# Joined: gate-row weights stacked as halves, a new order of the beginning, and turned weights evicted ahead of exponentials in the attention stage, with one weight split moved inside

## The reference, cut to what matters

```python
proj = x @ w_in                       # 1024 tokens, 1024 -> 5640 columns
(r_q, r_k, r_v, r_z, s_u, s_z, m_x, m_v, m_o, m_z, m_i, m_f, a_q, a_z) = split(proj)
...
y = gelu(y); s5o = y * sigmoid(y @ w_glu) * silu(s_z)          # S5 group, end of it
...
ig = m_i + ml_b_ig                                             # 4 gate rows
lf = log_sigmoid(m_f + ml_b_fg)                                # 4 gate rows
...
mk, mv = split(mem @ xa_w_kv)                                  # 256 memory tokens
s = einsum('blhd,bmhd->bhlm', a_q, mk) * XA_DH ** -0.5
xa = einsum('bhlm,bmhd->blhd', softmax(s), mv)                 # 4 heads
```

## Time and profile before

| | us |
|---|---|
| median of 3 runs | 1795.42 (1793.71 to 1797.22) |
| the profiled execution | 1792.38 |
| its span, first to last instruction | 1790.5 |
| PE busy | 1743.9 (97%) |
| DVE, ACT, POOL busy | 1026.6, 590.1, 545.0 |

### The profile page before, as it was taken

How to read it: one execution, slowest core, us unless ns; L and a number is a source line. 1 busy time by engine, 2 the same in 40 slices (tenths; PEclk the granted TensorE clock), 3 DMA queues, 4 the chain that set the end, 5 groups by cost and what they waited for, 6 DMA issues and landing times.

```text
span 1790.5 us, 22903 instructions
## 1 busy us (share of the span) xinstructions
PE 1743.9 (97%) x8880; PEld 1447.8 (81%) x8880; DVE 1026.6 (57%) x2018; ACT 590.1 (33%) x825; POOL 545.0 (30%) x354
## 2 busy tenths in 40 slices
PE   6999998999999999999999999989999999999998
PEld 6778886888787888888888788878887878888886
DVE  7899625562374378339747886243623925872524
ACT  5333343451124213432144332445211251143320
POOL 2553304022121413245455442130221131223451
PEclk9999999999999999999999999999999999999999
DMA  7334354042023206674433433640410322167451
GB/s 281 133 116 132 116 204 165 36 126 87 25 71 135 101 25 216 209 277 169 140 130 123 130 114 98 231 157 36 130 48 26 106 105 95 50 224 281 177 174 58
DMA packets 98707, 235.23 MB, mean 131 GB/s; under 512 B 10912, under 2 KB 41968, under 8 KB 97064
## 3 DMA queue, kind: packets, MB, share of 16 engines
q1 hardware_dynamic: 72744, 183.20, 30.2%
q10 hardware_dynamic: 25776, 50.34, 7.7%
q0 software_dynamic: 80, 0.23, 0.0%
HBM read 170.55 MB, written 58.98 MB: 128 GB/s over the span
## 4 chain that ended last, share of the span: by engine, by line
PE 81%; DVE 7%; DMA 4%; ACT 3%; POOL 2%; issue 1%; SPq 0%; ACTq 0%; DVEq 0%
PE gp L628 20%; PE gp L630 19%; PE gp L629 19%; PE mm L628 3%; PE mm L629 3%; PE mm L630 3%; POOL wlo L1144 2%; DMA wraw<-in_w 2%; PE mm L856 1%; PE mm L834 1%; PE mm L783 1%; DMA yraw<-yt 1%; PE mm L784 1%; PE mm L785 1%; PE mm L996 1%
## 5 line engine op out<-in xcount | busy, mean ns | idle before, releaser
L1144 POOL TENSOR_TENSOR wlo<-wraw,whi 128x256 fp32r<-128x256 f32 (+1 forms) x282 | 450.8, 1624 | 1037.6 <-ACT whi L1221 1037.4
L628 PE MATMUL gp<-xh,whi 128*128 128x512 f32 x768 | 320.3, 417 | 2.0 <-ACT xh L1288 1.1
L630 PE MATMUL gp<-xh,wlo 128*128 128x512 f32 x768 | 301.8, 393 | 0.0
L629 PE MATMUL gp<-xl,whi 128*128 128x512 f32 x768 | 300.7, 392 | 0.0
L628 PE MATMUL gp<-whi,xh 128*128 128x512 f32 x640 | 269.0, 420 | 0.0
L1221 ACT ACTIVATE whi<-wraw 128x1024 fp32r<-128x1024 f32 x164 | 168.2, 1054 | 294.4 <-DMA wraw<-in_w 132.2
L630 PE MATMUL gp<-whi,xl 128*128 128x512 f32 x640 | 250.5, 391 | 0.0
L629 PE MATMUL gp<-wlo,xh 128*128 128x512 f32 x640 | 250.0, 391 | 0.0
L630 PEld LDWEIGHTS gp<-xh,wlo 128*128 128x128 f32 x768 | 144.8, 189 | 32.1
L628 PEld LDWEIGHTS gp<-xh,whi 128*128 128x128 f32 x768 | 145.4, 189 | 31.1 <-issue 4.4
L629 PEld LDWEIGHTS gp<-xl,whi 128*128 128x128 f32 x768 | 145.7, 190 | 25.8
(11 more groups left out here) (333 smaller groups left out, 2942.0 us busy)
## 6 DMA issues: line engine op xcount, KB each, us to landing
wraw<-in_w SPq DMA_DIRECT2D x164, 512.0 KB, 4.1
spill<-gate ACTq DMA_DIRECT2D x32, 512.0 KB, 2.9
yraw<-yt SPq DMA_DIRECT2D x32, 512.0 KB, 5.5
xs<-xr SPq DMA_DIRECT2D x16, 512.0 KB, 5.4
xraw<-in_xT SPq DMA_DIRECT2D x4, 1024.0 KB, 17.9
ud<-gate ACTq DMA_DIRECT2D x8, 512.0 KB, 2.6
uu<-ud SPq DMA_DIRECT2D x64, 64.0 KB, 2.5
p_tab<-kd SPq DMA_DIRECT2D x64, 64.0 KB
```

The source lines that it names most:

```text
L628: nc.tensor.matmul(out, ah, bh, start=start, stop=False)
L629: nc.tensor.matmul(out, ah, bl, start=False, stop=False)
L630: return nc.tensor.matmul(out, al, bh, start=False, stop=stop)
L1144: last = nc.gpsimd.tensor_tensor(wlo[slot(u)][:, w0 + c:w0 + c + n], raw_view(l, u, i)[:, c:c + n], whi[slot(u)][:, w0 + c:w0 + c + n].bit ...
```

## The change

Four things.

1. **Gate rows.** `wif` is now held as one weight `wifs`: in each group of 128 columns, the high part stands in columns 0 to 63 and the low part in 64 to 127. Two matmuls (with the high and the low part of x) take the place of three, and leave the low weight's products in rows 64 to 67 and 96 to 99 of the result. ACT copies those rows out (`rowl`), and DVE adds them, two operations put between its third and fourth rotary operation. The order on ACT is rowb, a wait for the attention's last store (`xo_out`), the low rows of it, rowi, its low rows, and a wait for DVE's first addition, then abs, exp, ln.
2. **Attention.** In a hook that has both, ACT evicts turned weights ahead of exponentials. Of the split of U_QK + 1 the first half now stands in the U_GL + 1 part and the second at hook 7 of U_QK. ACT's first two stores of the S5 output stand after the evictions of U_GL + 1, and the second two at the hook of the first values. DVE's last product of the S5 gate stands behind the first maximum. U_QK leaves `SMALL_STEPS`.
3. **The beginning.** ACT issues the two loads of the memory; SP issues the S5 parameters, both halves of the first weight, and then the small constants, which count on `s_par` too. ACT's and DVE's first piece of work wait for both (32). DVE's step sizes are cut into three parts between the low parts, the 18 multiples and six operations of the second exp stand ahead of the low parts of x, and on ACT the high parts of x stand one place later, behind evictions.
4. **POOL** makes the two halves of U_SZ between its S5 rows, not behind them, in both layers.

The diff, cut to its core:

```diff
@@ names @@
-SMALL_STEPS = {U_SU[1], U_SZ, U_SZ + 1, U_AQ, U_AQ + 1, U_RZ, U_QK, U_QK + 1, U_AZ, U_AZ + 1}
+SMALL_STEPS = {U_SU[1], U_SZ, U_SZ + 1, U_AQ, U_AQ + 1, U_RZ, U_QK + 1, U_AZ, U_AZ + 1}
-        wifh, wifl = at("wifh", 1024, o_v + 3072, F32R), at("wifl", 1024, R[3] + 3072, F32R)
+        wifs = at("wifs", 1024, o_v + 3072, F32R)
+        rowl = [at(f"rowl{i}", T, R[1] + 2048 + T * i) for i in range(2)]
@@ SP @@
-            sp.dma_start(cst[:, K_MISC:K_COLS], dram["cst"][:, K_MISC:K_COLS]).then_inc(S["misc_in"], 16)
             sp.dma_start(s_in, dram["s5a"][0]).then_inc(S["s_par"], 16)
-            for i in range(2):
-                mem_load(i)
-                raw(0, U_MK, (i,))
+            raw(0, U_MK)
+            sp.dma_start(cst[:, K_MISC:K_COLS], dram["cst"][:, K_MISC:K_COLS]).then_inc(S["s_par"], 16)
@@ PE, gate rows @@
-                        last = mm3(mm[1][:, 512 * n:512 * n + 512], wifh[:, 128 * k:128 * k + 128], wifl[:, 128 * k:128 * k + 128],
-                                   xh[:, T * k + 512 * n:T * k + 512 * n + 512], xl[:, T * k + 512 * n:T * k + 512 * n + 512],
-                                   k == 0, k == KT - 1)
+                        for i, x in enumerate((xh, xl)):
+                            last = nc.tensor.matmul(mm[1][:, 512 * n:512 * n + 512], wifs[:, 128 * k:128 * k + 128],
+                                                    x[:, T * k + 512 * n:T * k + 512 * n + 512],
+                                                    start=k == 0 and i == 0, stop=k == KT - 1 and i == 1)
@@ POOL @@
                 rows(l, 0)
+                lo(l, U_SZ, (0,))
                 rows(l, 1)
-                lo(l, U_SZ)
+                lo(l, U_SZ, (1,))
@@ ACT, beginning @@
-            act.wait_ge(S["s_par"], 16)
+            for i in range(2):
+                act.dma_start(memraw[:, 1024 * i:1024 * i + 1024].rearrange("p (k m) -> p k m", k=4),
+                              dram["memT"][512 * i:512 * i + 512, :].rearrange("(k p) m -> p k m", p=128)).then_inc(mem_in[i], 16)
+            act.wait_ge(S["s_par"], 32)
...
                     split(l, U_MK + 1)
-                    x_split(0)
                     kv_evict(l, U_MK, 0)
                     kv_evict(l, U_MK, 1)
                     split(l, U_MV)
-                    x_split(1)
+                    x_split(0)
                     kv_evict(l, U_MK + 1, 0)
                     kv_evict(l, U_MK + 1, 1)
                     split(l, U_MV + 1)
+                    x_split(1)
                     x_split(2)
@@ ACT, end of S5 and attention @@
-                    if u == U_GL:
+                    if u == U_GL + 1:
+                        split(l, U_QK + 1, (0,))
                         for m in range(2):
-                            act.wait_ge(gate_used[m], NGATE * l + 1)
                             act.dma_start(dram["yt"][4 + m], sz[m]).then_inc(s5_out[m], 16)
...
+                    if hook in XT:
+                        x_turn(XT.index(hook))
                     if hook in XS:
                         x_exp(XS.index(hook))
-                    if hook in XT:
-                        x_turn(XT.index(hook))
...
+                    if hook == XV[0]:
+                        s5_store()
...
+                        if w == 0 and i == 7:
+                            split(l, u + 1, (1,))
@@ ACT, gate rows @@
-                F(rowi[0:4, :], mm[1][0:4, :], ACT.Identity, bias=small[0:4, 48:49]).then_inc(S["if_act"], 1)
-                A.link(F(rowb[0:4, :], mm[1][32:36, :], ACT.Identity, bias=small[0:4, 49:50]))
+                A.inc(F(rowb[0:4, :], mm[1][32:36, :], ACT.Identity, bias=small[0:4, 49:50]))
+                act.wait_ge(S["xo_out"], 64 * l + 64)
+                F(rowl[1][0:4, :], mm[1][96:100, :], ACT.Copy).then_inc(S["if_act"], 1)
+                A.inc(F(rowi[0:4, :], mm[1][0:4, :], ACT.Identity, bias=small[0:4, 48:49]))
+                F(rowl[0][0:4, :], mm[1][64:68, :], ACT.Copy).then_inc(S["if_act"], 1)
+                act.wait_ge(S["if_sum"], l + 1)
@@ DVE @@
-            step_sizes(0)
             for i in range(2):
+                step_sizes(0, i)
                 mem_split(0, i)
                 first_lo(U_MK, (i,))
+            step_sizes(0, 2)
+            first_lo(U_MK + 1)
             powers(0)
-            first_lo(U_MK + 1)
+            power_arguments(0)
...
+                    first_lo(U_MV)
                     x_low(0)
                     x_low(1)
-                    first_lo(U_MV)
-                    x_low(2)
-                    x_low(3)
                     first_lo(U_MV + 1)
-                    for k in range(4, KT):
+                    exp_reduce(s_mag, s_cos, s_sin)
+                    for k in range(2, KT):
                         x_low(k)
...
+                for m in range(3):
+                    s5_gate(m)
+                    s5_product(m)
+                s5_gate(3)
...
                         x_max(j)
+                        if j == 0:
+                            s5_product(3)
                         x_norm(j)
...
                 TT(ra, ra, rb, ALU.subtract).then_inc(S["rope_done"], 1)
+                dve.wait_ge(S["if_act"], 3 * l + 1)
+                TT(rowb[0:4, :], rowb[0:4, :], rowl[1][0:4, :], ALU.add).then_inc(S["if_sum"], 1)
+                dve.wait_ge(S["if_act"], 3 * l + 2)
+                V.inc(TT(rowi[0:4, :], rowi[0:4, :], rowl[0][0:4, :], ALU.add))
```

72 lines of the change are left out of this document (45 added, 27 removed).

## The result

The kernel after takes 1771.44 us, median of 4 runs (1769.98 to 1772.33); beside it the kernel before took 1794.57 (1790.97 to 1797.22). The ratio is 0.9874, 95% interval 0.986 to 0.9888: 23.1 us less, where 27.4 were forecast; the forecast time was 1768.0, and the range of 1761 to 1778 holds the result. The profiled execution is the fastest of the four, 1769.98 us, with a span of 1767.8, 22.7 less than before's 1790.5. Of the kernels further down one, `mem_on_sp`, had a single execution of 9962.12 us, which its time leaves out.

What follows compares the result with a forecast made beforehand. PE, busy 97% of the span, was taken as the bound. The terms 7.5 + 15.6 + 4.9 - 0.6 = 27.4 us came off the profiled 1792.4, giving 1765.0, or 1768.0 for the median; range 1761 to 1778.

Steps and rivals of the forecast that it cites:

- What bounds the kernel: Whole kernel: PE, busy 97% of the span; a matmul removed is time removed, other engines' edits give back only PE's idle time.
- Gate rows, 7.5: Gate rows, both layers: 32 matmuls for 48, 16 fewer at 0.235 us each, 3.75 us per layer, 7.5 us won.
- The thin cover of 2.5 us: Layer 0 gate rows: DVE's rows end at 411.0, PE comes to them at 413.5; a PE wait there was priced at nothing.
- Attention, 15.6: Attention, both layers: waits for exponentials (10.0) and `pt` (2.0) and two low-clock stretches (1.9 + 1.7) go, 15.6 us won.
- In front of S5, 4.9: Layer 0 before S5: wait for `p_ks` 2.3, POOL's low part 0.9 and low clock 1.7 go, 4.9 us won.
- 4 to 8 us come off the chain that ends in `p_ks`: DVE before S5: multiples and exp moved ahead of x's low parts shorten this chain, against 2.3 us that PE waits.
- m of 7.5: Beginning: time the small constants land, between 3.2 and 10.9, taken as 7.5; the second low part of U_MK then at 17.2.
- POOL's 0.9: Layer 0 before S5: POOL makes U_SZ's low part 5 us earlier, removing PE's wait of up to 0.9 us.
- The beginning, 0.6 lost: Beginning: 3.0 late, less 2.1 (`mkv`) and 1.7 (low clock), plus 1.0 and 0.4: 0.6 us lost; ends 3.7 won, 4.0 lost.
- The beginning is late: Rival: memory's second half lands 4 us later, `p_ks` no earlier relative to PE; 4 lost, half of 4.9 kept: 1774, chance 0.10.
- slower: Rival, attention: evicting turned weights first closes a loop of 4.0 us against PE's pace 4.8; at 6.0, 1799 us; chance 0.03.
- The other rivals: Attention still waits, 1776, chance 0.10; nothing comes of it, within 3.6 us, 0.03; more than the sum, 1763.7, 0.10.

Runs made afterwards that it cites:

- `mem_on_sp`: Kernel after, with SP's first loads in the old order (constants, S5 parameters, memory, weight, memory, weight), all from SP: 1765.9 us, ratio 0.9854.
- the one with the exp late: Kernel after with constants first on SP, and DVE's six operations of the second exp put back behind the low parts of x: 1766.28 us, ratio 0.9862.

## Why the prediction was right, step by step

- **What bounds the kernel.** Right. Matmuls removed were time removed, and all the rest came out of PE's idle time and clock.
- **Gate rows, 7.5.** Right: 3.75 in layer 0, and 7.8 for that part alone, 5.6 to 11.5 by its interval. The thin cover of 2.5 us held; DVE is done with `rk` at 401.28 + 1.22 = 402.5 and PE comes to it without a wait, 2.7 us later:

```profile
405.22 1.03 PE L890 MATMUL mm<-cst,rk 128*128 128x128 f32 x8
```

- **Attention, 15.6.** Right, and 1.7 us too small: 9.98 + 7.36 = 17.3 in the profile, counted behind the low clock, and 17.3 in the medians of that part alone. The two waits for `pm`, those for `pt` and both low stretches went, as priced. The reason named more than was needed: the step gave the half split at hook 7 and added the store, and each of the two would have done. The 2.0 for `pt` by the new order of ACT was measured as 2.8 in the rows and 5.4 in the medians. DVE's moved product, priced at tenths, and the large steps of U_QK were worth nothing by themselves; the large steps are a third cover against the same stall.
- **In front of S5, 4.9.** This term failed. Its step "4 to 8 us come off the chain that ends in `p_ks`" had the gain right and left out the cost: 7.9 us of DVE's idle time went, but the same chain begins with the constants, and DVE's start moved from 3.21 to 10.70, 7.5 us. By the prediction's own m of 7.5 that start was 4.3 us later, and it charged them to PE's beginning alone, as if `p_ks` were on another engine. So PE's wait for `p_ks` ended at 93.70 before and ends at 93.63 now. Of the three pieces only POOL's 0.9 came, as the wait of PE at 86.10 is gone, and it was waited away again. I had also written "the time to the loads behind `p_ks` is PE's own and stays", which is wrong: the restart comes 7.0 us after `p_ks`. Between its two waits PE worked 1.6 us less than before, at the higher level of the clock, and the second wait grew from 1.80 to 3.44. And the low clock is not gone; it now stands behind the second wait, at 100.68, and costs 1.6. Even with the constants first these two waits are 1.41 and 3.49.
- **The beginning, 0.6 lost.** The mechanism was right, and m was mis-sized: taken as 7.5, measured as 10.7, next to the bound of 10.9. The second low part came at 19.7, inside 13.3 to 20.6, where 17.2 was forecast. `mkv` fell as priced (2.1 to 0.7), and its low clock went (1.7). At the S5 tables' matmuls (83.19 before, 85.19 now) PE was 2.0 us late where 0.6 was forecast. The constants stood fourth in SP's queue behind 1 MB, and they landed at 10.6: in the middle was the wrong choice for a small load at the end of a queue.
- **Sum.** Beginning and S5 together were to bring 4.3 us. They brought 0.0 at 100.46 and lost 1.6 behind it. The attention brought 1.7 more than its 15.6, and 0.5 was lost between the layers: 27.4 - 4.3 - 1.6 + 1.7 - 0.5 = 22.7, which is what the span lost. So the forecast stands on two terms of four, gate rows and attention; the other two missed by 5.9 us, and that 1.7 came back from the attention is luck.
- **Rivals.** "The beginning is late" gave 1774 and had the right outcome at `p_ks`, "no earlier relative to PE". Its condition came true as well, the memory's second half landed late, at 12.3. But that held nothing up: ACT took it at 12.70 without a wait, and what was late were the constants. In "slower" the last sum is off: a loop of 6.0 us against the pace of 4.8 in 32 steps costs 38 us, so the time would be 1806 and not 1799; its semaphore delay of 0.3 us a pass is an assumption, where PE here follows `p_ks` by 0.15 (93.55 to 93.70). The loop never reached PE's pace, as the missing waits show. The other rivals did not occur.

The best version seen is the kernel after with its constants first, 1764.71 us, ratio 0.9835.

## What to carry to other kernels

When you move work ahead on an engine, write down one chain for it, from its first operation to the deadline: start, idle time, busy time. Filled gaps come off it (here 7.9 us of idle time), a later start goes on it (here 7.5), and where there is no gap to fill, the piece passed over is late next (here `zs`, 5.1 us). A small load that gates everything belongs ahead of the large ones in its queue; here its place was worth 5.0 us. And where a stall needs several conditions, undoing one is enough: undo the edits one at a time, and then together, before you say what each is worth.

## What the runs showed of the hardware

The moment at which PE's clock rises after its first matmul differs between runs that are alike up to there: matmuls stand 0.12 us apart from 14.8 on in the run with the constants first, and from 18.3 on in the one with the exp late, for first matmuls at 10.73 and 10.69. It moves what follows up to S5 by 1.1 to 1.6 us, and it is not bound to an edit: among six kernels with one and the same beginning the rise comes 4.3 us after the first matmul in two and 7.2 to 7.6 in four. The printed clock does not show it, as it reads 1.00 at both distances there. Compare two profiles from a common point behind it, not from the start.

A block of 8 KB, issued fourth in SP's queue behind 1 MB of weights and beside 1 MB on ACT's, landed 8.2 to 8.6 us after its issue in six traces; issued first it took 2.5 to 2.6 us beside the memory on ACT's queue (three traces) and 1.7 to 1.9 with the memory on SP's (five traces).
